# A mixture-of-experts block: the rows of a chunk picked out of on-chip tokens by products on TensorE

## The reference, cut to what matters

```python
for e in range(N_EXPERTS):                       # 16 experts, D = 1024, D_EXPERT = 512
    he = jax.nn.silu(t @ w_gate[e]) * (t @ w_up[e])
    y = y + gates[:, e:e + 1] * (he @ w_down[e])  # gates: two non-zeros per token
```

## Time and profile before

| | us |
|---|---|
| median of 3 runs | 1257.43 (1255.88 to 1260.43) |
| profiled execution, its own time | 1256.38 |
| its span, first to last instruction | 1254.4 |
| PE busy | 900.0 (72%) |
| DVE busy | 408.3 (33%) |
| ACT busy | 309.7 (25%) |
| POOL busy | 128.7 (10%) |
| mean granted TensorE clock | 0.883 |

### The profile page before, as it was taken

One profiled execution on the slowest core, in us unless ns is written; L12 is line 12 of the kernel. 1 busy time (PEld: TensorE's weight loads), 2 busy tenths in 40 slices (PEclk: granted clock), 3 DMA queues, 4 the chain that ended last, 5 costly groups with the idle time before them and its releaser, 6 DMA issues.

```text
span 1254.4 us, 22595 instructions
## 1 busy us (share of the span) xinstructions
PE 900.0 (72%) x8841; PEld 554.1 (44%) x8842; DVE 408.3 (33%) x1127; ACT 309.7 (25%) x703; POOL 128.7 (10%) x182
## 2 busy tenths in 40 slices
PE   5699989989962988797757438999973445436752
PEld 2244554434451655464434234865762223213432
DVE  1356655563243112111111144868342000001112
ACT  3322355552131111000000024247331111111211
POOL 1000000000003122211111120000002100100211
PEclk9899999999965999998888858999986877778995
DMA  8999599797033399999999973060334999999953
GB/s 307 400 366 318 179 386 328 261 344 269 0 134 145 115 336 334 342 333 343 330 351 350 362 258 123 1 216 3 135 134 175 350 378 371 358 367 381 335 173 110
DMA packets 144941, 329.25 MB, mean 262 GB/s; under 512 B 20528, under 2 KB 20800, under 8 KB 144896
## 3 DMA queue, kind: packets, MB, share of 16 engines
q1 hardware_dynamic: 118320, 295.41, 67.3%
q0 software_dynamic: 24864, 33.00, 8.6%
q10 hardware_dynamic: 1712, 0.23, 0.1%
HBM read 310.56 MB, written 35.65 MB: 276 GB/s over the span
## 4 chain that ended last, share of the span: by engine, by line
PE 37%; DMA 26%; SPq 11%; DVE 5%; issue 5%; ACT 3%; POOL 1%; POOLq 0%; ACTq 0%; DVEq 0%
DMA ring<-in_w_up_dram 12%; SPq L278 10%; PE bank L565 7%; DMA ring<-in_w_down_dram 7%; PE bank L522 7%; DMA h_t<-h_rows 5%; PE bank L422 3%; PE bank L577 3%; PE bank L492 3%; PE bank L365 3%; PE bank L463 2%; PE bank L475 2%; PE bank L533 1%; PE bank L431 1%; DVE h_t L1008 1%
## 5 line engine op out<-in xcount | busy, mean ns | idle before, releaser
L565 PE MATMUL bank<-ring,h_t 128*32 128x256 f32 x4160 | 273.7, 421 | 191.7 <-DMA ring<-in_w_up_dram 129.6
L565 PEld LDWEIGHTS bank<-ring,h_t 128*32 128x32 f32 x4160 | 164.7, 121 | 295.1 <-issue 181.9
L577 PE MATMUL bank<-ring,h_t 128*32 128x256 f32 x2080 | 125.5, 380 | 31.0 <-issue 19.4
L1157 DVE STREAM_TRANSPOSE h_t<-h_t 128x256 f32<-128x256 f32 x67 | 29.9, 446 | 306.8 <-PE bank L565 303.4
L422 PE MATMUL bank<-h_t,ring 128*128 128x512 f32 (+1 forms) x320 | 117.1, 521 | 12.3 <-ACT h_t L712 12.3
L799 ACT ACTIVATE h_t<-bank 128x128 f32<-128x128 f32 x65 | 18.1, 278 | 376.0 <-PE bank L565 376.0
L577 PEld LDWEIGHTS bank<-ring,h_t 128*32 128x32 f32 x2080 | 75.5, 110 | 72.7 <-issue 26.7
L924 POOL DMA_DIRECT2D y_rows<-work x66 | 46.3, 702 | 483.3 <-ACT work L805 391.2
L422 PEld LDWEIGHTS bank<-h_t,ring 128*128 128x128 f32 x320 | 62.0, 195 | 60.1 <-issue 40.5
L1153 DVE COPY h_t<-h_t 128x256 f32 (+1 forms) x71 | 21.0, 296 | 193.2 <-DMA h_t<-h_rows 187.9
L522 PE MATMUL bank<-tokm,ring 128*128 128x512 f32 (+1 forms) x256 | 83.1, 486 | 1.1 <-DVE tokm L1030 1.1
(11 more groups left out here) (147 smaller groups left out, 952.4 us busy)
## 6 DMA issues: line engine op xcount, KB each, us to landing
ring<-in_w_gate_dram SPq DMA_DIRECT2D x32, 2048.0 KB, 22.0
ring<-in_w_up_dram SPq DMA_DIRECT2D x32, 2048.0 KB, 26.8
ring<-in_w_down_dram SPq DMA_DIRECT2D x32, 2048.0 KB, 22.8
ring<-in_ada_w_dram SPq DMA_DIRECT2D x24, 2048.0 KB, 10.6
ring<-in_w_in_dram SPq DMA_DIRECT2D x8, 1536.0 KB, 22.1
h_t<-h_rows POOLq DMA_DIRECT2D x74, 128.0 KB, 8.7
h_rows<-in_table_dram SPq DMA_DIRECT2D x1, 9216.0 KB, 46.1
y_rows<-in_table_dram SPq DMA_DIRECT2D x1, 9216.0 KB, 68.3
```

The lines of the kernel that those rows point to most:

```text
L565: last = mm(o.rearrange("r (s c i) -> r s c i", s=2, c=KF), hc_t[:, k, :], w[:, :, k, :, CHUNK * q:CHUNK * q + CHUNK], start=(k == 0), sto ...
L577: last = mm(bank[4][CHUNK * q:CHUNK * q + CHUNK, 0:256], he_t[:, k, :], wd[:, k, 256 * q:256 * q + 256], start=(k == 0), stop=(k == KF - 1))
```

## The change

`h_rows` is gone, with its zeroing, the scatters and the loads. A chunk's rows are picked from `tokm` by a product: DVE builds, for chunk n, a 128x32 matrix per token tile that has a one where the token's row number equals 32 n + r (`hits` for both choices, then their sum `picks`), and PE multiplies `picks` (stationary) with `tokm` (moving) into `bank[5]`, accumulated over the token tiles. DVE transposes `bank[5]` directly into `hc_t`. PE runs `pick_rows` of the next chunk right behind each `gate_up`.

```diff
@@ PE
+                def pick_rows(n):
+                    pe.wait_ge(picks_ready[l], n + 1)
+                    for tt in range(nt):
+                        for q in range(4):
+                            last = mm(bank[5][CHUNK * q:CHUNK * q + CHUNK, 0:256], picks[:, tt, :],
+                                      tokm[:, tt, 256 * q:256 * q + 256], start=(tt == 0), stop=(tt == nt - 1))
+                    last.then_inc(rows_mm[l], 1)
@@ PE expert_long
                     gate_up(g0, a)
+                    pick_rows(g0 + 1)
                     if prev is not None:
                         down(g0 - 1, prev)
                     with pe.Fori(g0 + 1, g1) as g:
                         gate_up(g, a)
+                        pick_rows(g + 1)
                         weights_in(a, turns, (2,))
                         down(g - 1, a)
@@ PE expert_short
                         gate_up(g, a)
+                        pick_rows(g + 1)
                         weights_in(a, turns, (2,))
                         down(g, a)
...
                 pe.wait_ge(route_ready, l + 1)
+                pe.wait_ge(tok_ready, 2 * sum(TOK_TILES[:l + 1]))
+                pick_rows(0)
@@ POOL
-                pool.wait_ge(tok_ready, 2 * sum(TOK_TILES[:l + 1]))
-                pool.wait_ge(pos_ready, l + 1)
-                pool.wait_ge(rows_zeroed, 32)
-                for tt in range(nt):
-                    for s in range(2):
-                        pool.indirect_dma_start(h_rows[:, :], ...
-                pool.wait_ge(scattered, 32 * sum(TOK_TILES[:l + 1]))
+                pool.wait_ge(rows_zeroed, 16)
                 pool.wait_ge(route_ready, l + 1)
-                for n in range(4):
-                    if n >= 2:
-                        pool.wait_ge(hc_moved[l], n - 1)
-                    load_rows(n, n % 2)
...
                         pool.dma_start(y_rows[bass.ds(CHUNK * (2 * m + i), CHUNK), :] ...
-                        pool.wait_ge(hc_moved[l], 2 * m + 3 + i)
-                        load_rows(2 * m + 4 + i, i)
-                pool.wait_ge(hc_in[l][0], (total + 5) // 2 * 16)
-                pool.wait_ge(hc_in[l][1], (total + 5) // 2 * 16)
-                pool.wait_ge(hc_moved[l], total + 3)
+                pool.wait_ge(pos_ready, l + 1)
+                pool.wait_ge(picks_ready[l], total + 2)
@@ DVE
+                def pick(n):
+                    if not isinstance(n, int) or n > 0:
+                        dve.wait_ge(picks_ready[l], n)
+                    v.scalar_tensor_tensor(out=hits[:, 0:2 * nt], in0=pos[:, 0:2 * nt].unsqueeze(2).to_broadcast([P, 2 * nt, CHUNK]),
+                                           scalar=cst[:, bass.ds(n + C_G, 1)],
+                                           in1=cst[:, C_R:C_R + CHUNK].unsqueeze(1).to_broadcast([P, 2 * nt, CHUNK]),
+                                           op0=ALU.subtract, op1=ALU.is_equal).then_inc(hits_ready[l], 1)
+                    dve.wait_ge(hits_ready[l], n + 1)
+                    if not isinstance(n, int) or n > 0:
+                        dve.wait_ge(rows_mm[l], n)
+                    v.tensor_tensor(picks[:, 0:nt], hits[:, 0:nt], hits[:, nt:2 * nt], ALU.add
+                                    ).then_inc(picks_ready[l], 1)
+                def rows_turned(n):
+                    dve.wait_ge(rows_mm[l], n + 1)
+                    v.transpose(hc_t.rearrange("p k r -> p (k r)"), bank[5][:, 0:256]).then_inc(hc_ready[l], 1)
+                dve.wait_ge(pos_ready, l + 1)
+                pick(0)
+                rows_turned(0)
+                pick(1)
                 weights(l)
...
                 with dve.Fori(0, total) as g:
-                    dve.wait_ge(gu_mm[l], g + 1)
-                    rows_turned(g + 1)
                     dve.wait_ge(silu_done[l], g + 1)
                     v.tensor_tensor(he, act_g, bank[1][:, P:2 * P], ALU.mult).then_inc(he_ready[l], 1)
+                    if LEAST[l] > 1:
+                        dve.wait_ge(gu_mm[l], g + 1)
+                        rows_turned(g + 1)
                     dve.wait_ge(he_ready[l], g + 2)
                     dve.wait_ge(down_mm[l], g + 1)
                     v.transpose(he_t.rearrange("p k r -> p (k r)"), he).then_inc(het_ready[l], 1)
-                    rows_in(g + 2)
+                    if LEAST[l] == 1:
+                        dve.wait_ge(gu_mm[l], g + 1)
+                        rows_turned(g + 1)
+                    pick(g + 2)
```

More of the change, by code:

```diff
@@ L59 @@
 C_G = C_M1 + P
-C_TRI = C_G + MAXCH
+C_R = C_G + GT
+C_TRI = C_R + CHUNK
 C_W16 = C_TRI + (NE + 1) * NE
@@ L173, in backbone @@
         hflat = h_t[:, :, :].rearrange("p k n -> p (k n)")
-        hc_got = hflat[:, 0:512]
-        hc = hflat[:, 512:768]
+        picks = hflat[:, 0:128].rearrange("p (t r) -> p t r", t=4)
+        hits = hflat[:, 128:384].rearrange("p (m r) -> p m r", r=CHUNK)
         hc_t = hflat[:, 768:1024].rearrange("p (k r) -> p k r", k=KD)
@@ L211, in backbone @@
         rows_zeroed, block_zeroed = sem("rows_zeroed"), sem("block_zeroed")
-        hc_in = [[sem(f"hc_in{l}_{i}") for i in range(2)] for l in range(DEPTH)]
-        hc_moved, hc_ready = per_layer("hc_moved"), per_layer("hc_ready")
+        picks_ready, rows_mm, hc_ready = per_layer("picks_ready"), per_layer("rows_mm"), per_layer("hc_ready")
+        hits_ready = per_layer("hits_ready")
         gu_mm, silu_done, he_ready = per_layer("gu_mm"), per_layer("silu_done"), per_layer("he_ready")
@@ L299, in _ @@
                 if u == 5:
-                    for rows_dram in (h_rows, y_rows):
-                        sp.dma_start(rows_dram[0:ROWS, :].rearrange("(n p) d -> p n d", p=P),
-                                     table[:, C_Z:C_ALL].unsqueeze(1).to_broadcast([P, ROWS // P, D])
-                                     ).then_inc(rows_zeroed, 16)
+                    sp.dma_start(y_rows[0:ROWS, :].rearrange("(n p) d -> p n d", p=P),
+                                 table[:, C_Z:C_ALL].unsqueeze(1).to_broadcast([P, ROWS // P, D])
+                                 ).then_inc(rows_zeroed, 16)
                     sp.wait_ge(v_mm, 2)
@@ L1145, in route, with experts @@
                 v.tensor_copy(posidx[:, 0:2 * nt], pos[:, 0:2 * nt]).then_inc(pos_ready, 1)
[L1146 to L1162 removed]
+            def experts(l):
+                nt = TOK_TILES[l]
+                def pick(n):
[17 more added lines that the diff above has]
+                pick(1)
+                weights(l)
```

34 lines of the change are left out of this document (7 added, 27 removed).

## The result

The changed kernel takes 1200.63 us (median of 4 runs, 1193.17 to 1202.15) beside 1257.38 (4 runs, 1255.88 to 1260.43) for the kernel before: a ratio of 0.9534, with a 95% interval of 0.9491 to 0.9577, or 56.8 us less. The forecast was 49.4 us less and 1208 us, in a range of 1196 to 1232. The profiled execution is the shortest of the four: 1193.17 us, span 1191.4. Experiments are compared with it.

What follows compares the result with a forecast made beforehand. Both expert stages were taken as DMA bound behind their first experts, layer 0 turning PE bound. Layer 0 saves 21.3 us and layer 1 28.1, together 49.4, giving 1208 us in a range of 1196 to 1232.

Steps and rivals of the forecast that it cites:

- Start of layer 0: Layer 0's first `gate_up` starts at 390.9 us instead of 405.51 and takes 5.0 us (4.0 to 6.2).
- Pick and period: Each layer 0 chunk: a pick costs 1.73 us, as `down` does, making the period 6.91 us on PE.
- Rival A: Picks dearer than `down`, PE-bound layer 0: at 3.45 us a pick, 1286 us in all; chance 0.08.
- Rival B: Weight loads exposed in picks: 2.9 us a pick, 48 us more in layer 0, 1259 us, no change; chance 0.05.
- Rival C: Pick, turn and next `gate_up` in series: 0.6 to 0.8 us a chunk, 30 us, 1238 us; chance 0.11.
- New experts in layer 0: On PE in layer 0, 15 new experts cost a gap of 1.1 us each, 16.5 us together.
- No waits for weights in layer 0, clock 1.00: Layer 0 turns PE bound, 19.2 us per expert against 18.2 on DMA: no weight wait counted, clock 1.00 to the end.
- Start of layer 1: Layer 1's first `gate_up` comes 10.8 us earlier and is 0.3 us shorter, so the first refill comes 11.1 us earlier.
- The stream in layer 1: Up to expert 12's weights, 13 loads fewer at 0.8 us each save 10.4 us; steps of 17 us.
- Rival D: Loads cost only 0.33 us: 6 us less gain, layer 0's tail 4 instead of 9, 1219 us; 0.76 with forecast and E.
- E: Better: loads at 1.3 us, a first `gate_up` of 4.0, boundaries of 0.9: 1197 us; 0.76 with forecast and D.
- Last ten chunks, tail: Layer 1 after expert 12's wait: PE sets the pace, 6.28 us a chunk, 68.7 us together; tail saves 0.9 us.

Runs made afterwards that it cites:

- scatter_kept: The changed kernel with the scatters to DRAM back, unread, and the first pick waiting for them: 1221.98 us, ratio 0.9724.
- picks_looped: The changed kernel with every pick's products done twice, as a hardware loop of two turns over one copy of the code: 1280.68 us, ratio 1.0169.
- after: The profiled execution of the changed kernel in its first measurement, the shortest of four: 1193.17 us.
- loads_layer0: The changed kernel plus, in layer 0 alone, one 128 KB load per chunk that nobody waits for: 1211.51 us, ratio 0.9635.
- control: The changed kernel measured a second time, unedited: 1200.33 us, ratio 0.9542; its profiled execution took 1198.78 us.

## Why the prediction was right, step by step

- **Start of layer 0.** Right: 14.7 us earlier (14.6 forecast), and *scatter_kept* puts them back. The first `gate_up`, taken at 5.0 us, ran in 3.45 (granted clock 1.00 from 390.8 to 396.0): PE had worked through the pick before it. That is 1.5 us.
- **Pick and period.** Right to the last digit: 1.73 and 6.91 us, and *picks_looped* charges 1.73 for one more. The same-shape row of `down` was the right one to take, though the moving operand comes from `tokm`. Rival A (a dear pick) falls with it. Rival B falls too: the row shows 68 us of weight loads under 111 of matmuls at a step of 54 ns, all on the full 128 rows, in place of 90 ns. The Trainium skill's rule on row groups (TensorE: Matmul & The Clock Gate, Part 3), that a weight load overlaps matmuls in flight only when the row group differs, doesn't hold for these products on four column groups. The same part also lets a load into the background weight buffer go ahead, which would allow what the row shows; no run here can tell whether that is how it comes about. Rival C falls: 1.7 us of idle time on the turn in the whole kernel.
- **New experts in layer 0.** Taken at 1.1 us each from one row of before; the 15 of after average 0.89 (0.66 to 1.31, the larger where PE's loop turns back). The last product ended 4.5 us ahead of the forecast's 700.7: these two terms are 1.5 + 3.2, with 0.2 lost elsewhere.
- **No waits for weights in layer 0, clock 1.00.** Right, with more slack than the sum said (*loads_layer0*).
- **End of layer 0.** Right: 6.9 us from product to gather against 6.8.
- **Start of layer 1.** 10.8 us earlier than before relative to the gather was forecast. After `posidx` the first `gate_up` comes 3.45 us later in place of 13.92, 10.5 less. That `gate_up` took 4.12 us in one execution and 5.56 in the other, so its 0.3 us can't be judged.
- **The stream in layer 1.** The mechanism was right, the size was off. A load was taken at 0.8 us between bounds of 0.33 and 1.3, "an even split" of a pair's cost between load and store. It measures 1.24 to 1.41, on either side of the upper bound, and a store 0.37 to 0.44: nearly all of the pair's cost was the load's, and the even split was the mis-sized term. Thirteen loads at 0.45 more (1.25 less 0.8) are 5.9 us, the largest term of the 7.4 by which the medians beat the forecast. The step expected was 17 us, the one measured 16.3. Rival D (cheap loads) falls, E was the nearer one.
- **Last ten chunks, tail.** 70.0 us against 68.7 from expert 12's wait to the last product's end: a chunk there takes 6.48 us, not 6.28, as 0.24 us of issue remain ahead of `down`. The gather comes 11.6 us behind that end, where it was 12.7: 1.1 saved, 0.9 forecast.

The sum on the medians: 49.4 forecast; +1.5 and +3.2 (layer 0), +5.9 (loads), -1.3 (last chunks) make 58.7 against 56.8 measured. The 1.9 too many are less than one execution differs from the next (the control's from *after*'s: 5.6 us), so the small terms can't be told apart on this ground. The errors nearly all pointed one way, so the forecast wasn't right by terms that cancelled.

## What to carry to other kernels

A row gather through DRAM costs twice: its latency at the start of each stage, and its small reads as a tax on the weight stream, which is to be priced by a run or by the step between waits, not by its bytes.
## What the runs showed of the hardware

- A 128 KB load from DRAM in 1 KB pieces beside a saturated weight stream costs the stream 1.24 to 1.41 us, in 4 KB pieces 1.03, a store in 1 KB pieces 0.37 to 0.44, where their bytes at the stream's rate are 0.33. That reads cost about three times as much as writes of the same shape I hadn't expected; why isn't shown.
- A PE loop body of 1,920 instructions (matmul and weight-load records) stalls 7.2 to 8.1 us at each turn back, one of 1,536 about 0.6 us; the instruction queue shows it (76 packets against 33), and the line of the wait says only "issue".
- An fp32 product's record of 256 columns on four column groups costs 54 ns, a bf16 one 29, a bf16 one of 512 columns 56.
- POOL's TENSOR_TENSORs of 1.86 us stretch DVE's two-input instructions and a TENSOR_SCALAR of 0.17 to 0.22 us to 1.56 to 1.92, and leave a TENSOR_REDUCE at 0.22.
